# Two conditioning jobs of an encoder layer, each divided between TensorE and VectorE

## The chip, the cores and the metric

One NeuronCore of one Trainium2 chip runs the whole layer. The metric is the device time of one execution in microseconds. A *step* below is one 128x1024 slab of a weight matrix; a *unit* is one 512 KB load of the conditioning weights.

## The reference, cut to what matters

```python
c_act = jax.nn.silu(c)                                  # c: (1, 2048)
mod = c_act @ w_ada[0] + b_ada[0]                       # w_ada: (2048, 12288)
sh1, sc1, gt1, sh2, sc2, gt2 = jnp.split(mod, 6, axis=-1)
h = modulate(rms_norm(x, g_mix[0]), sh1, sc1)           # h * (1 + sc1) + sh1, 256 tokens x 2048
proj = h @ w_in[0] + b_in[0]                            # w_in: (2048, 5376)
# retention and windowed attention on proj, w_out, gt1, then the ConvGLU with sh2, sc2, gt2
fmod = c_act @ w_final_ada + b_final_ada                # shift and scale of the last norm
```

The conditioning vector `mod` is one row times a large matrix: 96 MB of weights for 12288 numbers. `h` needs `sh1` and `sc1` before `proj` can start on the features concerned.

## The kernel before, in words

Everything is float32 in memory. A product of the main path takes three TensorE passes over the halves of a split: ScalarE rounds a loaded slab into `whi` (`hi`, L643), VectorE writes the rest into `wlo` (`lo`, L999), TensorE multiplies (`passes`, L1535 to L1537). `whi` and `wlo` hold four steps each (RING = 4), so `hi(step)` waits until TensorE has done step - 4 or earlier. The raw slabs come through a ring of eight, loaded by SyncE (`load_step`, L365), each load issued once `lo` has freed or passed a given earlier step (for steps 16 to 37 once `lo(step - 6)` is done).

The projection is worked off while the conditioning vector is being made. The 2048 features are 16 tiles of 128 (`k`), and `STAGE_K` groups them into five stages: stage n needs the shift and scale of its own tiles, which conditioning *job* n gives. Stages 2 and 3, which the change touches, have twelve steps each: four of `att_queries(k)` and eight of `two_heads(stage, group, i)`, in four groups of query, heads, heads. In trace time stage 2 runs from about 83 to 129 us (steps 12 to 23 of the weights) and stage 3 from 129 to 174 us (steps 24 to 35). Each `two_heads` group fills PSUM banks 5 and 6; VectorE adds them to the running sum (`add_heads`, L1109) before the next group may write there (`bank_free`). So the heads of group 1 wait for `add_heads` of group 0, and so on.

A conditioning job 1, 2 or 3 makes 512 shifts and 512 scales. It has 16 units; unit k holds, in 128 partitions x 1024 columns, the rows of `w_ada` that belong to column k of `c_act`. TensorE takes them two at a time (`ada_pair(job, n)`, L1664): four fp32 matmuls of a 128x32 stationary tile `c_pad[:, k, :]`, recorded as eight instructions, in four column strips of the array. The strips collect in one PSUM bank; when eight pairs are done, VectorE adds the bias (`pe_rows`, L1031), TensorE sums the strips and turns them into columns (`sum_columns`, four matmuls against `pick`, L1608), and VectorE writes `mod_col` (`mod_cols`, L1049 and L1051), with which ScalarE modulates the next four tiles. Jobs 5 to 15 go another way: VectorE multiplies and accumulates a whole unit in one instruction (`ada_row`, L1009) and TensorE sums over partitions with a column of ones (L1611). The running sums lie in `acc`, four buffers of 128x1024.

In stages 2 and 3 the order written out by hand on TensorE is: in groups 0 and 1, query, pair, heads, pair, heads, pair; in group 2, query, heads, pair, heads, pair; in group 3, query, `sum_columns`, heads, heads. The order on VectorE, for i = 2 to 13: `lo_units(first + i)`, at i = 5, 8, 11 `add_heads` of groups 0, 1, 2, at i = 11 `pe_rows`, at i = 12 `mod_cols`; `first` is 12 and 24, so VectorE works at least two steps ahead.

GpSimd's queue issues the units, all from one instruction stream, in an order written out by hand (`pair_units`, `dve_unit`, L529), and clears and fills the bias of the `acc` buffers between them (`start_acc` L505, `next_acc`). Units of jobs 1 to 3 go round nine slots, eight of which (`k % 8`) these jobs use. A pair is issued when the pair four places earlier has been read:

```python
pool.wait_ge(ada_pe, PAIRS * job + n - (0 if job == JOB_SH2 else 3))
```

Of the kernel before, what the change touches and what calls it, by code (L numbers as in the profile page):

```python
# [25 lines left out]
ALU = mybir.AluOpType  # L26
ACT = mybir.ActivationFunctionType

P = 128
# [34 lines left out]
Y_PARTS = ((0, 0, GW), (0, GW, D), (1, 0, GW), (1, GW, GW + 512), (1, GW + 512, D))  # L64
ADA_PAIRS = 4


# [19 lines left out]
def build(nc, x, c, w_ada, b_ada, g_mix, w_in, b_in, sinks, w_out, g_ffn, w_up, w_conv, b_conv,  # L87
          w_down, w_final_ada, b_final_ada, g_final, rot, decay, masks, eye, out):
    ctx = ExitStack()
    with ctx:  # L90
# [177 lines left out]
        def rows_before(job):  # L268

            return KT * job - KT * JOB_DVE  # L270

# [4 lines left out]
        PAIRS = KT // 2  # L276

        def ada_slot(job, k):

            if job < 2:  # L280
                return k % (2 * RING)
            if job < JOB_SH2:
                return k % (2 * RING)
            if job == JOB_SH2:
                return PE_SLOTS[k % 2]
            n = rows_before(job) + k
            return n % RING
# [4 lines left out]
        def ada_value(job, k):  # L292

            if job < 2:
                return 16 * (2 * job + k // 8 + 1)
            if job < JOB_SH2:
                return 16 * (2 * job + k // (2 * RING) + 1)
            if job == JOB_SH2:
                return 16 * (2 * JOB_SH2 * (1 - k % 2) + k // 2 + 1)
            n = rows_before(job) + k  # L300
            return 16 * (2 * JOB_SH2 + n // RING + 1)

# [181 lines left out]
        def _(pool):  # L484
# [12 lines left out]
            def start_acc(job):  # L497

                a, col = acc[:, acc_of(job), :], column(job)
                before = [j for j in range(job) if acc_of(j) == acc_of(job)]  # L500
                if before and before[-1] < JOB_GT1:
                    pool.wait_ge(ada_red, summed(before[-1]))
                elif before:
                    pool.wait_ge(gt_ps, 2 * (before[-1] - JOB_GT1 + 1))
# [52 lines left out]
            def pair_units(job, n):  # L557

                if job == JOB_SH2 and n == 0:
                    pool.wait_ge(hlo_ready, KT)  # L560
                else:
                    pool.wait_ge(ada_pe, PAIRS * job + n - (0 if job == JOB_SH2 else 3))
                for k in (2 * n, 2 * n + 1):
                    load_unit(job, k, ada_slot(job, k))

            def dve_unit(n):

                job, k = JOB_DVE + n // KT, n % KT
                if n < RING:
                    pool.wait_ge(ada_pe, PAIRS * JOB_SH2 - RING + n // 2 + 1)  # L570
                else:
                    pool.wait_ge(ada_acc, n - RING + 1)
                load_unit(job, k, ada_slot(job, k))
# [23 lines left out]
            next_acc(3)  # L597
            for n in range(3):
                pair_units(2, n)
            next_acc(4)  # L600
            for n in range(3, PAIRS):
                pair_units(2, n)
            for n in range(3):
                pair_units(3, n)
            next_acc(5)
            for n in range(3, PAIRS):
                pair_units(3, n)
            for n in range(RING):
                dve_unit(n)
            pair_units(JOB_SH2, 0)  # L610
            next_acc(6)
            for n in range(RING, 3 * KT):
# [21 lines left out]
        def _(act):  # L634
# [168 lines left out]
            for p in range(P_WO):  # L803
# [9 lines left out]
                elif p == 25:  # L813

                    act.wait_ge(ada_pe, PAIRS * (JOB_SH2 + 1))
                    act.dma_start(dec, decay[:, :, 0:S]).then_inc(dec_in, 16)
                elif p in (30, 31):
                    exps(1, p - 30)
                elif 33 <= p < 37:
                    normalise(1, p - 33)  # L820
# [167 lines left out]
        def _(dve):  # L988
# [22 lines left out]
            def ada(job, k):  # L1011
# [5 lines left out]
                ada_row(acc[:, acc_of(job), :], ada_of_slot(ada_slot(job, k)), c_act[:, k:k + 1])  # L1017

            def first_rows(part):

# [5 lines left out]
            def pe_rows(job):  # L1026

                dve.wait_ge(bias_in, bias_value(job))
                dve.wait_ge(ada_pe, PAIRS * (job + 1))
                a = acc[:, acc_of(job), 0:512]  # L1030
# [117 lines left out]
            for stage in (2, 3):  # L1148
                first = AQ_STEPS[STAGE_K[stage][0]]
                for i in range(2, 14):  # L1150
                    lo_units(first + i)
                    if i in (5, 8, 11):
                        add_heads(stage, i // 3 - 1)
# [378 lines left out]
        def _(pe):  # L1532
# [68 lines left out]
            def sum_columns(job, bank, col0):  # L1601
# [3 lines left out]
                else:  # L1605
                    pe.wait_ge(ada_acc, rows_before(job + 1))
                for i in range(4 if job <= JOB_SH2 else 0):
                    last = nc.tensor.matmul(ps[:, bank, col0 + 2 * i:col0 + 2 * i + 2],  # L1608
                                            acc[:, acc_of(job), i * P:(i + 1) * P], pick[:, :], start=True, stop=True)
                for i in range(0 if job <= JOB_SH2 else 8):  # L1610
# [165 lines left out]
            for stage in (2, 3):  # L1776
                for group in range(4):
                    att_queries(STAGE_K[stage][group])
                    if group < 2:
                        ada_pair(stage, 3 * group)  # L1780
                    elif group == 3:
                        sum_columns(stage, ADA_BANK[stage], 0)
                    for i in range(2):
                        two_heads(stage, group, i)
                        if group < 3:
                            ada_pair(stage, 3 * group + i + (group < 2))
            keys_values(0)
# [253 lines left out]
```

## Time and profile before

| what | value |
|---|---|
| median of 3 runs | 1210.9 us (1209.73 to 1213.86) |
| the profiled execution's own time | 1214.22 us |
| its span, first to last instruction | 1212.5 us |
| mean granted TensorE clock | 0.988 |
| TensorE busy | 1176.8 us, 97% |
| VectorE busy | 899.0 us, 74% |

All times of rows are counted from the first instruction of the profiled execution, whose own time is 1.7 us above its span and 3.3 us above the median. "Busy" counts matmuls whose ends are modelled, so a full TensorE row says that its stream has no visible gap, and the distance between two starts is what an instruction group costs.

### The profile page before, as it was taken

The numbers are of one execution on the slowest core, as the hardware profiler recorded it, in microseconds if no ns is written. First come the engines' busy times: TensorE is split into PE (matmuls) and PEld (weight loads), VectorE is DVE, ScalarE is ACT, GpSimd is POOL, SyncE is SP. The second block draws the span as 40 slices with busy tenths as digits, with TensorE's granted clock in tenths as the row PEclk, the third lists the DMA queues.
The fourth block names the chain that finished last, engine by engine and source line by source line (L and its number), as shares of the span: only waits on it lengthen the run. The fifth ranks groups of instructions, "written<-read, shape, count | busy, mean of one in ns | idle before, by whom it ended". The sixth has DMA issues, their size and how long they took to land.

```text
span 1212.5 us, 19607 instructions
## 1 busy us (share of the span) xinstructions
PE 1176.8 (97%) x6800; PEld 986.4 (81%) x6800; DVE 899.0 (74%) x1111; ACT 656.3 (54%) x947; POOL 179.6 (15%) x307
## 2 busy tenths in 40 slices
PE   5999999999999999999999999999999999999995
PEld 3777898777888778888888888888888877888784
DVE  2444568998789887887887887877655666897886
ACT  5433344642754448565565665656655555555652
POOL 6342312221211110010111011000000000120101
PEclk9999999998999999999999999999999999999998
DMA  8999989998879984888888878885565557897841
GB/s 300 376 388 390 371 303 382 371 396 302 311 277 364 358 285 158 299 284 281 284 285 276 289 271 289 278 282 185 182 199 176 196 185 280 294 351 253 310 176 69
DMA packets 167478, 342.73 MB, mean 283 GB/s; under 512 B 10266, under 2 KB 103552, under 8 KB 166784
## 3 DMA queue, kind: packets, MB, share of 16 engines
q1 hardware_dynamic: 129072, 206.13, 49.1%
q0 software_dynamic: 37536, 134.30, 29.8%
q10 hardware_dynamic: 816, 1.58, 0.3%
q8 instruction: 34, 0.56, 0.2%
q14 instruction: 20, 0.16, 0.0%
HBM read 339.87 MB, written 2.10 MB: 282 GB/s over the span
## 4 chain that ended last, share of the span: by engine, by line
PE 83%; DMA 6%; DVE 5%; issue 2%; ACT 1%; POOL 1%; DVEq 0%; SPq 0%; ACTq 0%; POOLq 0%
PE ps L1559 27%; PE ps L1564 14%; PE ps L1535 13%; PE ps L1537 12%; PE ps L1536 12%; DMA ada_raw<-in_w_ada 3%; DVE acc L1009 2%; DMA raw<-in_w_in 2%; DMA arena<-in_w_ada 2%; PE ps L1664 2%; DVE wlo L999 1%; DVE xb L1333 1%; ACT whi L643 1%; PE ps L1611 0%; PE ps L1841 0%
## 5 line engine op out<-in xcount | busy, mean ns | idle before, releaser
L650 ACT ACTIVATE whi<-raw 128x1024 fp32r<-128x1024 f32 x256 | 271.6, 1062 | 286.4 <-PE ps L1564 180.6
L1004 DVE TENSOR_TENSOR wlo<-raw,whi 128x1024 fp32r<-128x1024 f32 x256 | 311.8, 1222 | 104.0 <-ACT whi L650 104.0
L1559 PE MATMUL ps<-hh,whi 128*128 128x512 f32 x1408 | 354.0, 393 | 0.0
L1559 PEld LDWEIGHTS ps<-hh,whi 128*128 128x128 f32 x1408 | 254.0, 189 | 45.9 <-issue 0.4
L1535 PE MATMUL ps<-whi,hh 128*128 128x512 f32 x608 | 243.1, 400 | 2.7 <-DVE wlo L999 1.4
L1537 PE MATMUL ps<-whi,hh 128*128 128x512 f32 x608 | 237.9, 391 | 0.0
L1536 PE MATMUL ps<-wlo,hh 128*128 128x512 f32 x608 | 237.7, 391 | 0.0
L643 ACT ACTIVATE whi<-raw 128x1024 fp32r<-128x1024 f32 x124 | 130.7, 1059 | 189.7 <-PE ps L1537 140.3
L1009 DVE SCALAR_TENSOR_TENSOR acc<-ada_raw,c_act,acc 128x1024 f32<-128x1024 f32 (+1 forms) x176 | 225.1, 1279 | 5.7 <-DMA ada_raw<-in_w_ada 5.0
L1564 PEld LDWEIGHTS ps<-hh,wlo 128*128 128x128 f32 x1408 | 192.1, 190 | 13.7
L999 DVE TENSOR_TENSOR wlo<-raw,whi 128x1024 fp32r<-128x1024 f32 x124 | 151.1, 1220 | 64.6 <-ACT whi L643 64.4
L1564 PE MATMUL ps<-hh,wlo 128*128 128x256 f32 x1408 | 196.3, 282 | 0.0
L1535 PEld LDWEIGHTS ps<-whi,hh 128*128 128x128 f32 x608 | 114.7, 189 | 34.3 <-issue 5.3
L1537 PEld LDWEIGHTS ps<-whi,hh 128*128 128x128 f32 x608 | 114.7, 189 | 24.7
L1536 PEld LDWEIGHTS ps<-wlo,hh 128*128 128x128 f32 x608 | 114.8, 189 | 23.5 <-issue 0.7
L529 POOL DMA_DIRECT2D ada_raw<-in_w_ada x136 | 76.3, 562 | 381.9 <-DVE acc L1009 328.5
L1535 PE MATMUL ps<-hh,whi 128*128 128x256 f32 x416 | 122.4, 294 | 3.2 <-DVE hh L1060 2.3
L1536 PE MATMUL ps<-hh,whi 128*128 128x256 f32 x416 | 118.5, 285 | 0.0
L1537 PE MATMUL ps<-hh,wlo 128*128 128x256 f32 x416 | 118.4, 285 | 0.0
L1535 PEld LDWEIGHTS ps<-hh,whi 128*128 128x128 f32 x416 | 81.5, 196 | 25.8 <-issue 25.8
L1536 PEld LDWEIGHTS ps<-hh,whi 128*128 128x128 f32 x416 | 81.7, 196 | 0.0
L1537 PEld LDWEIGHTS ps<-hh,wlo 128*128 128x128 f32 x416 | 81.6, 196 | 0.0
(161 smaller groups left out, 816.9 us busy)
## 6 DMA issues: line engine op xcount, KB each, us to landing
raw<-in_w_up SPq DMA_DIRECT2D x176, 512.0 KB, 4.4
ada_raw<-in_w_ada POOLq DMA_DIRECT2D x144, 512.0 KB, 7.2
raw<-in_w_down SPq DMA_DIRECT2D x44, 1024.0 KB, 6.5
ada_raw<-in_w_final_ada POOLq DMA_DIRECT2D x64, 512.0 KB, 5.3
raw<-in_w_in SPq DMA_DIRECT2D x52, 512.0 KB, 10.4
arena<-in_w_ada POOLq DMA_DIRECT2D x48, 512.0 KB, 9.1
raw<-in_w_in SPq DMA_DIRECT2D x16, 1024.0 KB, 8.8
raw<-in_w_out SPq DMA_DIRECT2D x16, 1024.0 KB, 8.1
```

The costliest lines, as they stand in the source:

```text
L529: pool.dma_start(dst, src).then_inc(ada_in[slot], 16)
L643: nc.scalar.activation(whi[:, step % RING, :], raw_of(step), ACT.Copy).then_inc(hi_ready, 1)
L650: nc.scalar.activation(whi[:, i % RING, :], raw_of(step0 + i), ACT.Copy).then_inc(hi_ready, 1)
L999: nc.vector.tensor_tensor(wlo[:, step % RING, :], raw_of(step), whi[:, step % RING, :], ALU.subtract).then_inc(lo_ready, 1)
L1004: nc.vector.tensor_tensor(wlo[:, i % RING, :], raw_of(step0 + i), whi[:, i % RING, :], ALU.subtract).then_inc(lo_ready, 1)
L1009: nc.vector.scalar_tensor_tensor(a, w, c_col, a, ALU.mult, ALU.add).then_inc(ada_acc, 1)
L1535: nc.tensor.matmul(out_ap, lhs[0], rhs[0], start=start, stop=False, skip_group_check=skip)
L1536: nc.tensor.matmul(out_ap, lhs[0], rhs[1], start=False, stop=False, skip_group_check=skip)
L1537: return nc.tensor.matmul(out_ap, lhs[1], rhs[0], start=False, stop=True, skip_group_check=skip)
L1559: nc.tensor.matmul(bank_of(m), whi[:, slot, tile(m, j)], hh[:, k0 + j, :, :].rearrange("p i s -> p (i s)"), start=start and j == 0, stop=F ...
L1564: last = nc.tensor.matmul(bank_of(m)[:, 0:S], wlo[:, slot, tile(m, j)], hhi[:, k0 + j, :], start=False, stop=True, skip_group_check=True)
L1664: last = nc.tensor.matmul(ps[row:row + 32, bank, :], c_pad[:, k, :], ada_of_slot(slot)[:, b * 512:(b + 1) * 512], start=n == 0, stop=True, ...
```

## The change

Jobs 2 and 3 are divided. TensorE takes units 0 to 7 as four pairs; VectorE takes units 8 to 15, one after each of `lo(first + 2)` to `lo(first + 9)`, into `acc` buffer 1 (`part_row`). `sum_columns` of these jobs gets eight more fp32 matmuls (128x128 of buffer 1 against one column of ones) that accumulate into the same eight PSUM columns. The order of TensorE in stages 2 and 3 becomes: in groups 0 and 1, query, heads, pair, heads, pair; in group 2, query, heads, heads; in group 3 as before. The eight slots are divided too: the pairs have four of them (so a pair is issued when the pair two places earlier has been read), VectorE's units the other four (a unit is issued when the row four places earlier is done). The order of GpSimd's queue becomes part, part, pair with both waits in one stream; the bias of buffer 1 for job 5 is moved behind job 3's sum, and the first four units of job 5 wait for rows of job 3.

```diff
--- before.py
+++ after.py
@@ -63,6 +63,7 @@
 LOOP = 8
 Y_PARTS = ((0, 0, GW), (0, GW, D), (1, 0, GW), (1, GW, GW + 512), (1, GW + 512, D))
 ADA_PAIRS = 4
+PART = 8
 
 
 JOB_SH2, JOB_SC2, JOB_GT1, JOB_GT2, JOB_FSC, JOB_FSH = 4, 6, 8, 10, 12, 14
@@ -267,20 +268,28 @@
 
         def rows_before(job):
 
-            return KT * job - KT * JOB_DVE
+            return KT * job - KT * JOB_DVE + 2 * PART
 
         def bias_value(job):
 
             return 32 * (job + 1) if type(job) is int and job <= JOB_SH2 else 16 * job + 16 * (JOB_DVE + 1)
 
         PAIRS = KT // 2
+
+        def pairs_before(job):
+
+            return PAIRS * job - PART // 2 * min(max(job - 2, 0), 2)
+
+        def part_before(job):
+
+            return PART * (job - 2)
 
         def ada_slot(job, k):
 
             if job < 2:
                 return k % (2 * RING)
             if job < JOB_SH2:
-                return k % (2 * RING)
+                return k % RING + (RING if k < KT - PART else 0)
             if job == JOB_SH2:
                 return PE_SLOTS[k % 2]
             n = rows_before(job) + k
@@ -294,11 +303,11 @@
             if job < 2:
                 return 16 * (2 * job + k // 8 + 1)
             if job < JOB_SH2:
-                return 16 * (2 * job + k // (2 * RING) + 1)
+                return 16 * (2 * job + k % PART // RING + 1)
             if job == JOB_SH2:
                 return 16 * (2 * JOB_SH2 * (1 - k % 2) + k // 2 + 1)
             n = rows_before(job) + k
-            return 16 * (2 * JOB_SH2 + n // RING + 1)
+            return 16 * (4 + n // RING + 1)
 
         def summed(job, part=1):
 
@@ -498,7 +507,9 @@
 
                 a, col = acc[:, acc_of(job), :], column(job)
                 before = [j for j in range(job) if acc_of(j) == acc_of(job)]
-                if before and before[-1] < JOB_GT1:
+                if job == JOB_DVE:
+                    pool.wait_ge(ada_red, summed(3))
+                elif before and before[-1] < JOB_GT1:
                     pool.wait_ge(ada_red, summed(before[-1]))
                 elif before:
                     pool.wait_ge(gt_ps, 2 * (before[-1] - JOB_GT1 + 1))
@@ -559,17 +570,22 @@
                 if job == JOB_SH2 and n == 0:
                     pool.wait_ge(hlo_ready, KT)
                 else:
-                    pool.wait_ge(ada_pe, PAIRS * job + n - (0 if job == JOB_SH2 else 3))
+                    pool.wait_ge(ada_pe, pairs_before(job) + n - (0 if job == JOB_SH2 else 1))
                 for k in (2 * n, 2 * n + 1):
                     load_unit(job, k, ada_slot(job, k))
 
+            def part_unit(job, i):
+
+                if job == 2 and i < RING:
+                    pool.wait_ge(ada_pe, pairs_before(2) - 3 + i // 2)
+                else:
+                    pool.wait_ge(ada_acc, part_before(job) + i - RING + 1)
+                load_unit(job, KT - PART + i, ada_slot(job, KT - PART + i))
+
             def dve_unit(n):
 
                 job, k = JOB_DVE + n // KT, n % KT
-                if n < RING:
-                    pool.wait_ge(ada_pe, PAIRS * JOB_SH2 - RING + n // 2 + 1)
-                else:
-                    pool.wait_ge(ada_acc, n - RING + 1)
+                pool.wait_ge(ada_acc, 2 * PART + n - RING + 1)
                 load_unit(job, k, ada_slot(job, k))
 
             nc.gpsimd.memset(c_pad[:, :, :], 0.0).then_inc(pad_zero, 1)
@@ -595,19 +611,23 @@
             next_acc(2)
             eight_units(1, 1)
             next_acc(3)
-            for n in range(3):
+            for i in range(RING):
+                part_unit(2, i)
+            for n in range(2):
                 pair_units(2, n)
-            next_acc(4)
-            for n in range(3, PAIRS):
+            for n in range(2, 4):
+                part_unit(2, 2 * n)
+                part_unit(2, 2 * n + 1)
                 pair_units(2, n)
-            for n in range(3):
-                pair_units(3, n)
-            next_acc(5)
-            for n in range(3, PAIRS):
+            for n in range(4):
+                part_unit(3, 2 * n)
+                part_unit(3, 2 * n + 1)
                 pair_units(3, n)
             for n in range(RING):
                 dve_unit(n)
+            next_acc(4)
             pair_units(JOB_SH2, 0)
+            next_acc(5)
             next_acc(6)
             for n in range(RING, 3 * KT):
                 for pair in range(1, PAIRS):
@@ -812,7 +832,7 @@
                     normalise(0, p - 14)
                 elif p == 25:
 
-                    act.wait_ge(ada_pe, PAIRS * (JOB_SH2 + 1))
+                    act.wait_ge(ada_pe, pairs_before(JOB_SH2 + 1))
                     act.dma_start(dec, decay[:, :, 0:S]).then_inc(dec_in, 16)
                 elif p in (30, 31):
                     exps(1, p - 30)
@@ -1016,6 +1036,18 @@
                     dve.wait_ge(ada_acc, rows_before(job) + k)
                 ada_row(acc[:, acc_of(job), :], ada_of_slot(ada_slot(job, k)), c_act[:, k:k + 1])
 
+            def part_row(job, i):
+
+                k, n = KT - PART + i, part_before(job) + i
+                w, col = ada_of_slot(ada_slot(job, k)), c_act[:, k:k + 1]
+                dve.wait_ge(ada_in[ada_slot(job, k)], ada_value(job, k))
+                if i:
+                    dve.wait_ge(ada_acc, n)
+                    ada_row(acc[:, 1, :], w, col)
+                else:
+                    dve.wait_ge(ada_red, summed(job - 1))
+                    nc.vector.tensor_scalar(acc[:, 1, :], w, col, None, ALU.mult).then_inc(ada_acc, 1)
+
             def first_rows(part):
 
                 dve.wait_ge(bias_in, bias_value(0))
@@ -1026,7 +1058,7 @@
             def pe_rows(job):
 
                 dve.wait_ge(bias_in, bias_value(job))
-                dve.wait_ge(ada_pe, PAIRS * (job + 1))
+                dve.wait_ge(ada_pe, pairs_before(job + 1))
                 a = acc[:, acc_of(job), 0:512]
                 nc.vector.tensor_tensor(a, ps[:, ADA_BANK[job], :], a, ALU.add).then_inc(ada_rows, 1)
 
@@ -1149,6 +1181,8 @@
                 first = AQ_STEPS[STAGE_K[stage][0]]
                 for i in range(2, 14):
                     lo_units(first + i)
+                    if i < 2 + PART:
+                        part_row(stage, i - 2)
                     if i in (5, 8, 11):
                         add_heads(stage, i // 3 - 1)
                     if i == 11:
@@ -1604,9 +1638,16 @@
                     pe.wait_ge(ada_rows, summed(job))
                 else:
                     pe.wait_ge(ada_acc, rows_before(job + 1))
+                if job in (2, 3):
+                    pe.wait_ge(ada_acc, part_before(job + 1))
                 for i in range(4 if job <= JOB_SH2 else 0):
                     last = nc.tensor.matmul(ps[:, bank, col0 + 2 * i:col0 + 2 * i + 2],
-                                            acc[:, acc_of(job), i * P:(i + 1) * P], pick[:, :], start=True, stop=True)
+                                            acc[:, acc_of(job), i * P:(i + 1) * P], pick[:, :], start=True,
+                                            stop=job not in (2, 3), skip_group_check=True)
+                    for b in range(2 if job in (2, 3) else 0):
+                        last = nc.tensor.matmul(ps[:, bank, col0 + 2 * i + b:col0 + 2 * i + b + 1],
+                                                acc[:, 1, (4 * b + i) * P:(4 * b + i + 1) * P], ones[:, 0:1],
+                                                start=False, stop=b == 1, skip_group_check=True)
                 for i in range(0 if job <= JOB_SH2 else 8):
                     last = nc.tensor.matmul(ps[:, bank, col0 + i:col0 + i + 1], acc[:, acc_of(job), i * P:(i + 1) * P],
                                             ones[:, 0:1], start=True, stop=True)
@@ -1776,14 +1817,12 @@
             for stage in (2, 3):
                 for group in range(4):
                     att_queries(STAGE_K[stage][group])
-                    if group < 2:
-                        ada_pair(stage, 3 * group)
-                    elif group == 3:
+                    if group == 3:
                         sum_columns(stage, ADA_BANK[stage], 0)
                     for i in range(2):
                         two_heads(stage, group, i)
-                        if group < 3:
-                            ada_pair(stage, 3 * group + i + (group < 2))
+                        if group < 2:
+                            ada_pair(stage, 2 * group + i)
             keys_values(0)
             keys_values(1)
             for k in STAGE_K[4]:
```

## Rows read from the trace of the kernel before

**Rows 1.** The page: busy time of two engines, and shares of the last chain by engine.
```profile
PE 1176.8 (97%) x6800; PEld 986.4 (81%) x6800; DVE 899.0 (74%) x1111; ACT 656.3 (54%) x947; POOL 179.6 (15%) x307
PE 83%; DMA 6%; DVE 5%; issue 2%; ACT 1%; POOL 1%; DVEq 0%; SPq 0%; ACTq 0%; POOLq 0%
```
**Rows 2.** Windows: length, busy PE, PEld, DVE, ACT, POOL, granted clock, DMA share, GB/s.
```profile
80.00:100.00 20.00, 19.49 (x156) 15.50 (x155) 9.78 (x14) 9.04 (x14) 7.12 (x10) 1.00 1.04 389
100.00:130.00 30.00, 29.68 (x239) 25.78 (x240) 16.04 (x23) 13.13 (x18) 8.52 (x12) 1.00 1.03 390
130.00:140.00 10.00, 10.00 (x82) 8.06 (x81) 5.38 (x6) 2.92 (x3) 2.81 (x4) 1.00 0.95 343
165.00:190.00 25.00, 25.00 (x211) 25.00 (x211) 20.18 (x24) 12.15 (x16) 5.31 (x10) 1.00 0.82 270
190.00:285.00 95.00, 90.24 (x655) 70.79 (x655) 85.52 (x120) 46.84 (x96) 21.34 (x41) 1.00 1.00 388
```
**Rows 3.** The chain that ended last, 60 to 260 us: start, length, what.
```profile
76.69 20.55 DMA raw<-in_w_in
97.26 1.07 ACT whi L643
...
99.49 0.70 DVE xb L1109
...
100.32 0.36 PE ps L1535
...
198.37 0.13 PE ps L1537
```
**Rows 4.** Timeline of PE in stages 2 and 3: start, length.
```profile
100.32 0.36 PE L1535 MATMUL ps<-hh,whi 128*128 128x256 f32 x1 [0.42 <-DVE xb L1109]
...
108.45 0.39 PE L1535 MATMUL ps<-hh,whi 128*128 128x256 f32 x1
...
122.41 1.05 PE L1608 MATMUL ps<-pick,acc 128*128 128x2 f32 x8
...
123.33 0.37 PE L1535 MATMUL ps<-hh,whi 128*128 128x256 f32 x1
...
129.17 0.28 PE L1535 MATMUL ps<-hh,whi 128*128 128x256 f32 x1
...
133.13 0.39 PE L1535 MATMUL ps<-hh,whi 128*128 128x256 f32 x1
...
137.21 0.39 PE L1535 MATMUL ps<-hh,whi 128*128 128x256 f32 x1
...
174.10 0.28 PE L1535 MATMUL ps<-hh,whi 128*128 128x256 f32 x1
```
**Rows 5.** The chain of waits: eight and sixteen instructions against one column of ones.
```profile
50.55 0.78 PE ps L1635 x8
...
287.88 2.19 PE ps L1611 x16
```
**Rows 6.** Timeline of DVE in stages 2 and 3, and in stage 4.
```profile
98.35 1.23 DVE L999 TENSOR_TENSOR wlo<-raw,whi 128x1024 fp32r<-128x1024 f32 x1 [1.98 <-ACT whi L643]
...
121.68 0.68 DVE L1031 TENSOR_TENSOR acc<-ps,acc 128x512 f32<-128x512 f32 x1
...
176.64 1.28 DVE L1009 SCALAR_TENSOR_TENSOR acc<-ada_raw,c_act,acc 128x1024 f32<-128x1024 f32 x1
177.84 1.22 DVE L999 TENSOR_TENSOR wlo<-raw,whi 128x1024 fp32r<-128x1024 f32 x1
...
195.59 1.22 DVE L999 TENSOR_TENSOR wlo<-raw,whi 128x1024 fp32r<-128x1024 f32 x1 [3.30 <-ACT whi L643]
```
**Rows 7.** Timeline of POOL: units issued (L529) and a buffer cleared (L505).
```profile
82.28 1.42 POOL L529 DMA_DIRECT2D arena<-in_w_ada  x2
87.58 1.41 POOL L529 DMA_DIRECT2D ada_raw<-in_w_ada  x2 [3.88 <-PE ps L1664]
...
174.51 0.97 POOL L505 MEMSET acc<- 128x1024 f32 x1
```
**Rows 8.** Landing of the units issued 78 to 110 us, then of those issued 138 to 156 us.
```profile
DMA to landing us min/median/max: 8.4/9.4/11.2
...
DMA to landing us min/median/max: 6.6/7.9/11.6
```
**Rows 9.** Waits from 76 to 124 us: engine, line, waited for; total, times, longest.
```profile
ACT whi L643 <- DMA raw<-in_w_in: 24.1, 11, 3.1
```

## The prediction

> **What bounds the kernel now.** The page comes first: TensorE is busy 97% of the span and holds 83% of the chain that ended last, while VectorE is busy 74% [rows 1]. Work taken from TensorE is worth something only where the chain runs through TensorE, so the next views are the chain and the windows of the two stages that change. Up to 100.32 us the chain is not on TensorE: it comes from the load of a weight slab, step 17, 20.55 us in flight, through ScalarE's rounding of it at 97.26, VectorE's `lo(17)` at 98.35 and the `add_heads` queued behind it at 99.49, which frees the banks for step 16 on TensorE at 100.32 [rows 3, 6]. From there to 198.37 us the chain is TensorE's [rows 3]. The windows say why: from 80 to 130 us the DMA engines are full (share 1.03 to 1.04, 389 GB/s) and TensorE is nearly full too, 19.49 of 20 and 29.68 of 30 us; from 130 us the transfers have caught up (0.95, later 0.82) and TensorE alone is full [rows 2]. ScalarE waits 24.1 us for slabs in stage 2 [rows 9]. So stage 3 is bound by TensorE, and stage 2 by TensorE with the transfers close behind.
>
> **What is removed: eight pairs.** A step behind a pair and before one costs 137.21 - 133.13 = 4.08 us [rows 4]. Stage 3 as a whole, twelve steps, eight pairs and a sum, takes 174.10 - 129.17 = 44.93 us [rows 4]; a step without a pair is 2.88 us (from 123.33 to 129.17, two steps, the first 0.08 longer because it comes behind fp32 matmuls: 5.84 [rows 4]). A pair therefore costs 4.08 - 2.88 = 1.20 us. Check: 12 x 2.88 + 8 x 1.20 = 44.2, and 0.8 to 0.9 for the sum makes 45.0. Stage 3 loses four pairs, 4.8 us. Stage 2 loses four as well, but two of them stood ahead of step 16, where TensorE then waits for the slab anyway [rows 3]. Only two, 2.4 us, are on the path.
>
> **What is added on TensorE: eight matmuls in each sum.** They are recorded as sixteen instructions. The same shape costs 0.78 us for eight [rows 5], so 1.6 us for sixteen, or 2.2 us as in the later sum of sixteen [rows 5]. I take 1.7, nearer to the first, because the clock is 1.00 in both stages [rows 2]. Two jobs: 3.4 us, range 3.2 to 4.4, all on the path. Without any new wait the change is thus worth 4.8 + 2.4 - 3.4 = 3.8 us.
>
> **What is added on VectorE: sixteen rows.** Row to next instruction is 177.84 - 176.64 = 1.20 us [rows 6], so 9.6 us in each stage. VectorE is busy 9.78 of 20 and 16.04 of 30 us in stage 2 [rows 2]; a step with its share of pairs takes TensorE over 3 us and VectorE needs 1.2 for `lo`, 1.2 for the row: hidden, except where `add_heads` stands behind a row. That is so for step 16, whose banks wait for `lo(17)`, then row 3, then `add_heads`: 1.2 us on the path if slab 17 lands when it did. But between 82.28 and 87.58 us four units are issued [rows 7] that the new order issues only after row 0 and row 1 (the slots are not free sooner), some 91 to 95 us. That is 2.1 MB, 5.4 us of all DMA engines at 389 GB/s [rows 2]; about half has come back by 97 us. Slab 17 lands 1.4 to 2.7 us earlier, 2.0 taken. Net: step 16 starts 0.8 us earlier, at 99.5 us; bounds 1.6 earlier (TensorE is ready no sooner) and 1.2 later.
>
> **What is moved: the units.** A pair now has four slots and stands behind two of VectorE's units in GpSimd's one queue. Pair 2 of stage 2 is behind the part that waits for row 1: with row 1 done at about 93 us, its second unit is issued at 94.4. Units issued here take 8.4 to 11.2 us to land, 9.4 in the middle [rows 8], so it is there at 103.8. TensorE wants it after step 16, at 99.5 + 2.9 = 102.4: a wait of 1.4 us. With pair 2 (1.2) and step 17 (2.9) TensorE is at 107.9. Pair 3 is behind the part that waits for row 3, done at 98.6 (before `add_heads`, 0.7, and 99.5); its second unit is issued at 100.0 and lands at 109.4, a wait of 1.5 us. Step 18 starts at 110.6 where it was 108.45 [rows 4]. From there four steps without pairs, 11.6 us, lead to the sum at 122.2, as now (122.41 [rows 4]). The sum can't be much earlier: `pe_rows`, 0.68 us from 121.68 [rows 6], is behind slab 23 and `add_heads`. It takes 0.9 + 1.7, so heads follow at 124.9 against 123.33: **stage 2 is 1.6 us longer.**
>
> In stage 3, starting at 130.8 us, row 1 is done at 136.7. Pair 2 is issued once pair 0 is done, by 138.3, lands 7.9 us later [rows 8] at 146.2 and is wanted at 147.6. Pair 3, issued at 142.6 behind row 3, lands at 150.5 and is wanted at 151.7. No wait by the middle landing, up to 2.5 us by the longest, 11.6 [rows 8]. So **stage 3 is shorter by 4.8 - 1.7 = 3.1 us.**
>
> Here a rule speaks against these waits: the Trainium skill, DMA: Bandwidth & Descriptors, section "Anatomy of one DMA — SWDGE (gpsimd) path", gives a transfer issued by GpSimd about 2.0 us plus its bytes at 436 GB/s, 3.2 us for a unit. By it both waits of stage 2 would be gone (2.9 us), the first rival below; the trace shows more than twice that wherever the engines are full, and the measurement decides here.
>
> **Behind the stages.** Buffer 1 is cleared for job 5 only after job 3's sum, and two more clearings with a wait for a bias between them stand in GpSimd's queue before the fifth unit of job 5; before, one clearing stood there at 174.51 [rows 7]. I estimate that unit 2 to 3 us late. VectorE's row 4 then waits as long, and behind it `lo`; TensorE is some steps behind, and VectorE has 3.30 us without work at 192 to 195.6 us [rows 6] that takes it up. If that cover were gone it would cost up to 3 us. DMA share 0.82 from 165 to 190 us [rows 2] leaves the transfers room to follow a small shift; from 190 to 285 us they are full again, 1.00 [rows 2], and could swallow a gain, not a loss.
>
> **The sum.** + 1.6 - 3.1 = -1.5 us. On the profiled execution, 1214.2 becomes 1212.7; on the median, which is 3.3 us lower, 1210.9 becomes about 1209.4.
>
> **The rivals.**
> 1. *Units land in time* (faster). No waits at pairs 2 and 3 and step 16 up to 1.6 us earlier: 3.8 + 1.6 = 5.4 us off, 1208.8 for the profiled execution and 1205.5 for the median. For it: no unit is issued from about 80 to 91 us, so that later ones may find the engines emptier. Against it: with 9.4 us landing and an issue hardly 8 us ahead the two waits follow from arithmetic, and the sum is held by slab 23.
> 2. *GpSimd's queue makes the pairs late* (slower). The point is the landing time: at 11.2 us in stage 2, and slab 17 no earlier than now, step 16 starts at 101.5; pair 2, issued at 95.1, waits 1.9 us, pair 3, issued at 102.3, 3.1 us. Step 18 then starts at 114.7, the sum 11.6 later at 126.3, and the heads behind it at 128.9, 5.6 us late. Stage 3, with 2.5 us of waiting, gains only 0.6. Together 5.0 us slower, 1215.9.
> 3. *Nothing passes through*: the transfers, full to 130 and again from 190 us [rows 2], bring the slabs at the times they do now, and 1.5 to 3 us won on TensorE are spent waiting: 1211.
>
> **How the numbers follow.** About 0.3%, 3.6 us, is what a measurement of this kernel can tell from no change. Forecast with its near neighbours (gain of 0 to 3.6 us) 0.42; rival 1 beyond 3.6 us 0.20; rival 3 and small losses 0.18; rival 2 beyond 3.6 us 0.20. Faster 0.20, same 0.60, slower 0.20. Range 1205.5 to 1216: from rival 1 to rival 2.
>
> **What would show it.** the pairs' line with 192 instead of 256 instructions; 14 more instructions of the accumulating row (the first of each job only multiplies); sums of about 2.6 us near 122 and 164 us; TensorE idle before two pairs between 100 and 110 us, released by a load of `w_ada`; step 18 later than 108.45 us, and stage 3 about 41.8 us long with no idle time. The prediction is wrong if landing in stage 2 leaves 9.4 us by more than 1.5, if a sum costs over 3.1 us, if slab 17 doesn't move, or if VectorE comes to wait for its own units and holds `lo` back.

## The result, and the profile after

The changed kernel takes 1223.36 us (median of 4 runs, 1222.0 to 1224.02) against 1210.56 us for the kernel before: ratio 1.0096, 95% interval 1.0069 to 1.0123. It is slower by 8 to 15 us where 1.5 us faster was forecast, and outside the range.

The page of the changed kernel, the lines of [rows 1]. TensorE has 32 instructions fewer (64 of the pairs gone, 32 in the sums new) and 1.7 us less busy time in a span that is 8.7 us longer. (The medians differ by 12.8 us: the profiled execution of the kernel before was 3.3 us above its median, that of the changed kernel 0.5 us below.)

```profile
PE 1175.1 (96%) x6768; PEld 988.2 (81%) x6768; DVE 916.7 (75%) x1127; ACT 656.5 (54%) x947; POOL 179.7 (15%) x307
PE 83%; DMA 7%; DVE 5%; issue 2%; ACT 1%; POOL 1%; DVEq 0%; SPq 0%; ACTq 0%; POOLq 0%
```

The windows of the changed kernel, columns as in [rows 2]:

```profile
80.00:100.00 20.00, 17.53 (x140) 15.25 (x140) 14.72 (x20) 11.06 (x15) 4.50 (x7) 1.00 1.04 390
100.00:130.00 30.00, 24.57 (x163) 19.86 (x161) 16.10 (x16) 5.47 (x6) 6.77 (x10) 0.89 1.02 383
130.00:140.00 10.00, 10.00 (x86) 10.00 (x86) 4.93 (x10) 6.66 (x11) 0.00 (x0) 1.00 0.39 117
140.00:165.00 25.00, 21.98 (x161) 16.31 (x160) 20.37 (x20) 6.36 (x6) 7.49 (x12) 1.00 0.91 322
```

TensorE was busy 29.68 of 30 us from 100 to 130 us [rows 2] and is now busy 24.57, at a granted clock of 0.89 instead of 1.00. From 130 to 140 us the DMA engines move 117 GB/s where they moved 343 [rows 2]. TensorE's timeline through the two stages, to be held against [rows 4], says where:

```profile
99.48 0.37 PE L1569 MATMUL ps<-hh,whi 128*128 128x256 f32 x1 [1.06 <-DVE xb L1141]
...
103.33 1.05 PE L1705 MATMUL ps<-arena,c_pad 128*32 128x512 f32 x4 [0.73 <-DMA arena<-in_w_ada]
105.36 1.05 PE L1705 MATMUL ps<-arena,c_pad 128*32 128x512 f32 x4 [0.98 <-DMA arena<-in_w_ada]
106.35 0.39 PE L1569 MATMUL ps<-hh,whi 128*128 128x256 f32 x1
...
112.14 1.05 PE L1705 MATMUL ps<-arena,c_pad 128*32 128x512 f32 x4 [2.64 <-DMA arena<-in_w_ada]
114.27 1.92 PE L1705 MATMUL ps<-arena,c_pad 128*32 128x512 f32 x4 [1.08 <-DMA arena<-in_w_ada]
116.12 0.58 PE L1569 MATMUL ps<-hh,whi 128*128 128x256 f32 x1
...
120.94 0.28 PE L1569 MATMUL ps<-hh,whi 128*128 128x256 f32 x1
...
132.17 0.37 PE L1569 MATMUL ps<-hh,whi 128*128 128x256 f32 x1
...
138.02 0.28 PE L1569 MATMUL ps<-hh,whi 128*128 128x256 f32 x1
...
162.34 1.05 PE L1705 MATMUL ps<-arena,c_pad 128*32 128x512 f32 x4 [1.50 <-DMA arena<-in_w_ada]
164.12 1.05 PE L1705 MATMUL ps<-arena,c_pad 128*32 128x512 f32 x4 [0.73 <-DMA arena<-in_w_ada]
165.10 0.39 PE L1569 MATMUL ps<-hh,whi 128*128 128x256 f32 x1
...
185.14 0.28 PE L1569 MATMUL ps<-hh,whi 128*128 128x256 f32 x1
```

Three things are to be seen. Step 16 starts at 99.48 us, as forecast. The late pairs shown are recorded as two groups of four instructions, one for each unit, with a gap ahead of both, released by the load of that unit (pair 2 of stage 3 waits 0.80 us for its second unit alone). And pair 3 of stage 2 with its waits holds TensorE from the end of step 17, near 109.3, to 116.12 us. Stage 3 begins at 138.02 instead of 129.17 and ends at 185.14 instead of 174.10 [rows 4]: 11.0 us are lost by then.

The chain that ended last now runs, just ahead of 114 us, through exactly the queue that was in question (start, length, what):

```profile
97.45 1.29 DVE acc L1029
98.74 0.29 issue
99.03 0.70 POOL ada_raw L540
99.73 0.69 POOL arena L540
100.42 13.80 DMA arena<-in_w_ada
114.22 0.04 issue
114.27 1.92 PE ps L1705 x4
```

VectorE's row 3, then GpSimd's issue of VectorE's unit, then of the pair's, then 13.80 us of transfer, then TensorE. GpSimd's timeline shows the pause and the burst behind it, against two units at 82.28 and two at 87.58 in [rows 7]:

```profile
77.04 2.80 POOL L540 DMA_DIRECT2D arena<-in_w_ada  x4 [2.67 <-PE ps L1705]
90.53 0.71 POOL L540 DMA_DIRECT2D ada_raw<-in_w_ada  x1 [10.69 <-DVE acc L1049]
93.69 0.71 POOL L540 DMA_DIRECT2D ada_raw<-in_w_ada  x1 [2.45 <-DVE acc L1029]
94.39 0.71 POOL L540 DMA_DIRECT2D arena<-in_w_ada  x1
...
99.72 1.41 POOL L540 DMA_DIRECT2D arena<-in_w_ada  x2
...
141.60 0.71 POOL L540 DMA_DIRECT2D ada_raw<-in_w_ada  x1 [23.69 <-DVE acc L1049]
```

Eight units are issued in the 10 us from 90.53, one each 1.4 us, where before it was two each 4.1 us. Ahead of stage 3 GpSimd waits 23.69 us for row 0 of the fourth job. Its last unit has landed at 130.0 us, and SyncE, whose slabs wait for VectorE's splits and so for TensorE, issues a single one between 130 and 140 us: the DMA engines run nearly dry.

### The profile page after: what moved, and what is told of

Its sections match the earlier page's. It is cut to its first block, busy times and chain, and to the rows that moved or that the text cites. A ratio compares the mean times of both kernels' runs of the same rounds, so it can differ in the third digit from the quotient of the medians.

```text
span 1221.2 us, 19577 instructions
## 1 busy us (share of the span) xinstructions
PE 1175.1 (96%) x6768; PEld 988.2 (81%) x6768; DVE 916.7 (75%) x1127; ACT 656.5 (54%) x947; POOL 179.7 (15%) x307
## 4 chain that ended last, share of the span: by engine, by line
PE 83%; DMA 7%; DVE 5%; issue 2%; ACT 1%; POOL 1%; DVEq 0%; SPq 0%; ACTq 0%; POOLq 0%
PE ps L1593 27%; PE ps L1598 14%; PE ps L1569 13%; PE ps L1571 12%; PE ps L1570 12%; DMA arena<-in_w_ada 4%; DVE acc L1029 2%; DMA raw<-in_w_in 2%; DMA ada_raw<-in_w_ada 2%; PE ps L1705 1%; DVE wlo L1019 1%; ACT whi L663 1%; DVE xb L1367 1%; PE ps L1652 0%; PE ps L1880 0%
## 5 line engine op out<-in xcount | busy, mean ns | idle before, releaser
L1029 DVE SCALAR_TENSOR_TENSOR acc<-ada_raw,c_act,acc 128x1024 f32<-128x1024 f32 (+1 forms) x190 | 242.9, 1279 | 7.9 <-DMA ada_raw<-in_w_ada 7.1
L1569 PEld LDWEIGHTS ps<-whi,hh 128*128 128x128 f32 x608 | 114.3, 188 | 34.4 <-issue 5.3
## 6 DMA issues: line engine op xcount, KB each, us to landing
raw<-in_w_in SPq DMA_DIRECT2D x52, 512.0 KB, 10.7
```

Of the source, the lines that this page charges most:

```text
L1029: nc.vector.scalar_tensor_tensor(a, w, c_col, a, ALU.mult, ALU.add).then_inc(ada_acc, 1)
L1569: nc.tensor.matmul(out_ap, lhs[0], rhs[0], start=start, stop=False, skip_group_check=skip)
```

## The experiments

Theory L: the units of pairs 2 and 3 are issued too late, because they stand behind VectorE's rows in one queue with only four slots, and TensorE stands idle for them. Rivals: R, VectorE's rows hold back the splitting of the slabs; D, the transfers as a whole are the limit. Lengths below: stage 2 from the heads behind job 1's sum (80.26 us before, 79.76 changed) to stage 3's first step; before 48.9 us, changed 58.3; stage 3 before 44.9, changed 47.1. Every ratio is to the kernel before, run beside the kernel in question; its median was 1210.56 to 1211.68 us from one comparison to the next, so a difference in microseconds between two of them can be off by about 1 us.

### Late pairs

```diff
-                        if group < 2:
-                            ada_pair(stage, 2 * group + i)
+                        if group == 0:
+                            ada_pair(stage, i)
+                        elif group == 2 and i:
+                            ada_pair(stage, 3)
```
and `ada_pair(stage, 2)` behind the query of group 2.

> The changed kernel with pairs 2 and 3 of each shared job later in TensorE's order: pair 2 behind the query of group 2, pair 3 behind the second heads of group 2 (before: both in group 1). Nothing else moves. Theory L (the units of pairs 2 and 3 are issued too late behind VectorE's units in GpSimd's queue, and TensorE stands idle for them): the waits before these pairs all but vanish, stage 3 starts 6 to 9 us earlier than in the changed kernel, and the time falls by 8 to 12 us to some 1212 to 1215. Rival R (VectorE's rows hold back the splitting of the slabs): no change, 1223. Rival D (the transfers as a whole are the limit): under 3 us gained.

Measured: 1209.56 us, ratio 0.9979 (0.9963 to 0.9994). The waits at pairs are gone from the trace, though the units land no sooner. Landing of those issued from 97 to 102 us, in this kernel:

```profile
DMA to landing us min/median/max: 10.2/14.0/14.7
```

The same late units cost nothing if TensorE asks for them two or three steps later (pair 3's second unit lands at 114.51 us and is used at 114.59). Stage 3 takes 172.42 - 130.46 = 41.96 us, the 41.8 of the forecast. L holds, though the gain is 13.8 us where it expected 8 to 12; R and D fall, since all rows and all loads are still there. Only a move in TensorE's order turns a loss of 1% into a gain of 0.2%.

### Pairs first in GpSimd's queue

```diff
-                part_unit(2, 2 * n)
-                part_unit(2, 2 * n + 1)
                 pair_units(2, n)
+                part_unit(2, 2 * n)
+                part_unit(2, 2 * n + 1)
```
and the same for the fourth job.

> The changed kernel with each pair's two units issued ahead of VectorE's two units in GpSimd's queue, where they stood behind. Theory L: pairs 2 and 3 of stage 2 are issued about 3 and 4 us earlier and wait that much less, in both stages; 1223 becomes 1214 to 1218. Rival B (the units land late because ten of them are issued in 10 us after a pause, whatever their order): the waits only move from the pairs to the rows, and less than 3 us is gained. Rival R: no change.

Measured: 1218.35 us, ratio 1.0061 (1.0038 to 1.0085), 5 us better than changed. The wait moves from TensorE to VectorE, which now waits four times, up to 5.5 us, for its own units (waits from 76 to 190 us: total, times, longest):

```profile
DVE acc L1029 <- DMA ada_raw<-in_w_ada: 14.7, 4, 5.5
PE ps L1705 <- DMA arena<-in_w_ada: 3.8, 4, 1.3
```

In the changed kernel these rows are 3.2 us (2 times) and 8.5 us (7 times). The gain lies between the two expectations. About a third of what the waits cost (5.0 of 14.7 us, the next experiment) is the order of VectorE's units and the pairs in the queue.

### No wait at the late pairs

```diff
+                    held = job in (2, 3) and n >= 2
+                    if not held:
-                    pe.wait_ge(ada_in[slot], ada_value(job, k))
+                        pe.wait_ge(ada_in[slot], ada_value(job, k))
```
and the moving operand of a held pair is `c_pad`. TensorE waits for the held units only ahead of the sum. The kernel leaves these eight units out of the conditioning vector.

> The changed kernel in which pairs 2 and 3 of the two shared jobs multiply a constant tile that is always there; their units are still loaded, and TensorE waits for them only at the sum. It leaves these eight units out of the conditioning vector. Theory L: all of the idle time before these pairs is gone, about 5.4 us in stage 2, 3 us in stage 3 and what the fallen clock cost; 1223 becomes 1209 to 1212. Rival R: it stays above 1218, since the rows remain. Rival D: slabs arrive no sooner and stage 2 ends within 2 us of where it did.

Measured: 1208.65 us, ratio 0.9975 (0.9962 to 0.9987): 14.7 us below the changed kernel. TensorE has no gap from 100 to 130 us:

```profile
100.00:130.00 30.00, 30.00 (x237) 28.06 (x237) 19.71 (x26) 12.23 (x16) 6.07 (x9) 0.94 1.03 389
```

So the waits and what follows from them are the whole loss. It is also a measured value of the change without them: 0.25% faster, 3.0 us (1.6 to 4.6), near the 3.8 us of the prediction's sum without new waits, though this trace has the clock at 0.94 in the stretch.

### Narrow rows

```diff
-                    ada_row(acc[:, 1, :], w, col)
+                    ada_row(acc[:, 1, 0:8], w[:, 0:8], col)
```
(and the first row likewise). The kernel leaves the rest of VectorE's share out.

> The changed kernel with VectorE's sixteen rows cut to 8 of 1024 columns, all waits and loads kept. It leaves the rest of VectorE's share out. Theory L: the rows themselves cost nearly nothing, since the pairs wait for loads; but each load behind a row is issued about 1 us earlier, so 1 to 3 us are gained, 1220 to 1222. Rival R: the loss goes with them, 1211 to 1214.

Measured: 1219.79 us, ratio 1.0082 (1.0065 to 1.0099), 3.6 us less than changed, with overlapping intervals. TensorE still waits, for units that release it at 103.1, 105.2 and 114.1 us; in the changed kernel it was at 103.3, 105.4 and 114.3. R falls as a main cause. Pair 3's units are issued 2.0 us earlier (97.77 against 99.72 us) and land no earlier.

### A fill under the wait

```diff
+                        if stage == 2 and group == 1 and i:
+                            for _ in range(5):
+                                nc.tensor.matmul(ps[:, 7, :], ident[:, :], c_pad[:, :, :].rearrange("p k c -> p (k c)"),
+                                                 start=True, stop=True, skip_group_check=True)
```

> The changed kernel with five fp32 matmuls of the identity against a constant tile, into a PSUM bank that nobody reads, ahead of pair 3 of stage 2, where TensorE stands idle. Theory C (the half clock from 114 to 120 us follows from the idle time before it): the fill hides under the wait, the clock stays at 1.00, step 18 starts where it did and step 19 some 2 us sooner behind it; stage 3 starts 2 to 3.5 us earlier. Rival: the clock falls at about this time whatever TensorE does, and stage 3 starts where it did or later.

The granted clock in the changed kernel, and in this one:

```profile
114.00:116.00 2.00, 1.73 (x4) 0.19 (x4) 0.00 (x0) 0.00 (x0) 0.15 (x1) 0.50 1.04 387
116.00:118.00 2.00, 2.00 (x11) 1.88 (x10) 0.00 (x0) 0.00 (x0) 1.40 (x2) 0.50 1.04 390
118.00:120.00 2.00, 2.00 (x11) 2.00 (x11) 0.00 (x0) 0.00 (x0) 0.00 (x0) 0.50 1.03 389
```

```profile
114.00:120.00 6.00, 5.18 (x39) 4.10 (x38) 0.00 (x0) 0.72 (x1) 1.40 (x2) 1.00 1.04 390
130.00:134.00 4.00, 4.00 (x23) 4.00 (x22) 2.50 (x6) 3.08 (x7) 0.00 (x0) 0.57 0.59 176
```

The first fence is the changed kernel, the second the one with the fill. With the fill, which takes 4.45 us from 108.80 us, the 1.2 GHz level (0.50) is gone at 114 us, and step 18 takes 2.97 instead of 4.82 us. The sum starts 1.9 us earlier, at 127.66. But the low level comes behind the sum instead, at 130 us, and takes most of that back: stage 3 starts at 137.59, where it was 138.02. There is one time, 1221.34 us, which can't be told from 1223. So half of the expectation holds in this one execution: with the idle time filled, the clock does not fall at 114 us. The gain is missing, because it then falls behind the sum.

### Early rows in stage 2

```diff
             mod_cols(1, ADA_BANK[1], 0)
+            for i in range(2):
+                part_row(2, i)
```
and rows 2 to 7 behind the splits of steps 14 to 19.

> The changed kernel with VectorE's rows of stage 2 two places earlier: rows 0 and 1 straight behind the second job's columns, near 81 us, the others behind the splits of steps 14 to 19. Theory B (the units of pairs 2 and 3 land late because GpSimd stops for 10.7 us at row 0 and then issues eight units in 10 us, one each 1.2 us, where the full engines land one each 2.1 us): the landing of pair 3's units falls from 12.4 to 13.8 us to some 9, step 18 starts 4 to 6 us earlier, the clock does not fall there, and the time is 5 to 9 us below 1223. Rival (a longer landing comes from the four slots alone): under 2 us gained, since pair 3 is still issued only behind pair 1.

Measured: 1219.22 us, ratio 1.0068 (1.0045 to 1.0092), 4 us less. Pair 3 is issued at 95.77 instead of 99.72 us and lands at 108.2 and 110.4 instead of 112.1 and 114.3, so its landing time did not fall:

```profile
DMA to landing us min/median/max: 11.0/13.8/15.3
```

(units issued from 95 to 101 us). The intervals of this kernel and the changed one overlap. The clock does not fall at pair 3, but in the profiled execution it does behind the sum, from 126.8 us. Theory B, that spreading the issue brings landing back to 9 us, is not confirmed: six units, pair 3's the last of them, are still issued between 91.7 and 96.5 us. A kernel without any burst was not tried.

### The sum alone, on the kernel before

```diff
+                    for b in range(2 if job in (2, 3) else 0):
+                        last = nc.tensor.matmul(ps[:, bank, 8 + 2 * i + b:8 + 2 * i + b + 1],
+                                                acc[:, acc_of(job), i * P:(i + 1) * P], ones[:, 0:1],
+                                                start=True, stop=True, skip_group_check=True)
```

> The kernel before, with the eight one-column matmuls added to the sums of jobs 2 and 3 (on a buffer that is there, into columns that nobody reads) and nothing else of the change. The forecast's term: 1.7 us each, 3.4 us in all, 1214. Theory C2: one or two stretches at half clock on top, 2 to 3.4 us each, so 1216 to 1221.

Measured: 1217.28 us, ratio 1.0045 (1.0028 to 1.0063): 3.4 to 7.6 us. The sums take 2.69 and 2.75 us from start to the next step, 0.8 to 0.9 before. Behind the second one the clock falls:

```profile
168.00:170.00 2.00, 2.00 (x21) 2.00 (x19) 0.00 (x0) 1.06 (x1) 0.00 (x0) 1.00 0.83 220
170.00:172.00 2.00, 2.00 (x13) 2.00 (x13) 1.02 (x3) 0.63 (x2) 0.00 (x0) 0.61 0.17 66
172.00:174.00 2.00, 2.00 (x11) 2.00 (x11) 1.27 (x3) 1.94 (x5) 0.00 (x0) 0.53 0.23 28
```

Steps 34 and 35 behind it take 7.20 us instead of the 5.84 of the two steps from 123.33 us before [rows 4]. This longer sum costs its instructions, 1.8 to 1.9 us each time, and in the profiled execution 1.4 us at the low clock on top, behind one of the two sums. How often that happens in the other five executions isn't known.

### The sum in two parts

Late pairs, and VectorE's part of the sum ahead of the last query of the stage, TensorE's part behind it:

```diff
                 for group in range(4):
+                    if group == 3:
+                        sum_part(stage)
                     att_queries(STAGE_K[stage][group])
```
(The waits and banks that go with it are left out here.) In the first version every column of VectorE's part set the start flag, and that kernel leaves part of the sum out; the second sets it once for the bank and leaves nothing out.

> The kernel with the late pairs and the sum cut in two: the sixteen instructions on VectorE's part stand ahead of the last query of the stage, the eight on TensorE's part behind it, both into a bank of their own. Theory C2 (a 2.6 us stretch of twenty-four matmuls of one or two columns brings the half clock seen from 120.6 to 127.6 us in the kernel with late pairs, as it does behind the sum of jobs 4 and 5 in the kernel before): no half clock in stage 2, 2 to 3.4 us gained, ratio to before some 0.996. Rival (the clock falls there for another reason): the same half clock within 5 us, ratio 0.998.

> The kernel with late pairs and the divided sum once more, with one start flag for the bank, so that both parts add up. The same instructions and waits: ratio 0.996 again, and a fall of the clock of no more than 4 us in stage 2.

Measured: 1207.4 us, ratio 0.9962 (0.9948 to 0.9976), and 1207.98 us, 0.9972 (0.9960 to 0.9984). In the profiled execution of the first the clock falls all the same, right behind the sixteen instructions:

```profile
118.00:122.00 4.00, 4.00 (x23) 4.00 (x23) 1.32 (x2) 0.00 (x0) 0.00 (x0) 0.57 1.04 395
```

In that of the second it stays at 1.00 through both stages; yet that execution, 1212.84 us, was the longest of its twelve. The intervals of both overlap that of the late pairs alone. That the divided sum helps is not shown.

### Early rows, late pairs and the divided sum together

No edit of its own: the three above in one kernel.

> Late pairs, divided sum, and VectorE's rows of stage 2 two places earlier, together. If the early rows help beside the late pairs (units spread better), ratio 0.993 to 0.995. If they only bring slab 17 and step 16 later, as they did alone (100.6 against 99.5 us), and no pair waits any more, 0.996 to 0.998.

Measured: 1209.45 us, ratio 0.9982 (0.9970 to 0.9994). Once no pair waits, early rows bring nothing that can be seen; step 16 starts at 100.05 us. In the profiled execution the clock falls twice in stage 2, from 89.0 and from 119.7 us, each time for 3.4 us.

### One job at a time

The third job alone shared, with the changed order in stage 2, and the fourth alone:

```diff
-                        if i < 2 + PART:
+                        if stage == 2 and i < 2 + PART:
```
(and the counts, slots and TensorE's and GpSimd's orders of the other job as before).

> Only the third job is shared, with the changed kernel's order of TensorE and GpSimd in stage 2; the fourth job and stage 3 are as before. Stage 2 was 9.3 us longer in the changed kernel and stage 3 2.2 us longer, so theory L expects 7 to 10 us above before, 1218 to 1221, with the waits at pairs 2 and 3 of stage 2 and the half clock behind them. Rival (the loss needs both jobs, through the one second sum): under 5 us.

> Only the fourth job is shared, with the changed kernel's order in stage 3; the third job and stage 2 are as before. The first four units of VectorE's part and two pairs are on their way in stage 2, but unit 4 of its part still waits for row 0 behind the split of step 26. Theory L: waits of 2 to 4 us at pairs 2 and 3 against 3.1 us saved, so 1210 to 1215. The forecast's walk of stage 3 (no waits): 1208. With a half clock behind the longer sum, 2 us more.

Measured: third alone 1220.3 us, ratio 1.0084 (1.0063 to 1.0105); fourth alone 1214.31 us, 1.0036 (1.0021 to 1.0051). Their sum is 1.2%, in the interval of the whole. In the third alone, stage 2 takes 58.2 us and stage 3 44.9; pair 3 waits as in the changed kernel:

```profile
111.89 1.05 PE L1714 MATMUL ps<-arena,c_pad 128*32 128x512 f32 x4 [2.64 <-DMA arena<-in_w_ada]
114.02 1.92 PE L1714 MATMUL ps<-arena,c_pad 128*32 128x512 f32 x4 [1.07 <-DMA arena<-in_w_ada]
```

In the fourth alone stage 2 is as before and stage 3 takes 46.7 us, with gaps ahead of both units of pair 3:

```profile
153.11 1.05 PE L1707 MATMUL ps<-arena,c_pad 128*32 128x512 f32 x4 [1.41 <-DMA arena<-in_w_ada]
154.89 1.05 PE L1707 MATMUL ps<-arena,c_pad 128*32 128x512 f32 x4 [0.72 <-DMA arena<-in_w_ada]
```

Each stage makes its own loss; the shared second sum between the jobs isn't needed for it.

## Why the prediction was wrong

**What failed** is the step "units issued here take 8.4 to 11.2 us to land, 9.4 in the middle" and its twin with 7.9 us in stage 3. The landing time was read from a kernel that issues two units each 4.1 us and carried over, as if it were a property of the transfer, to one that stops for 10.7 us and then issues eight in 10 us. Pair 3's second unit took 13.80 us in stage 2 and 14.0 in stage 3. I named the landing time as the point on which rival 2 turns, but set its upper end at 11.2, the longest before, so that the bound was too low as well. The sign that I gave for it, a landing more than 1.5 us off 9.4, is there.

**Why it took 13.80 us.** The landing of each single unit can be read from the traces. In every kernel here GpSimd's units land, from 76 to 190 us, in the order in which they were issued, and while the engines are full, about one each 2.1 us: pair 3's two units and the five before them at 101.16, 103.29, 105.32, 107.44, 109.69, 112.09 and 114.22 us, a mean distance of 2.2; in the kernel before, from 98.59 to 111.41 us, 2.1. So the landing time is mostly a place in the line. Of the units issued in the changed kernel from 95.67 us on, the one with three loads of GpSimd's still under way took 9.65 us, those with four 10.7, the one with five 12.4, and pair 3's second unit, with six, 13.80. In the kernel before there were never more than five from 78 to 110 us. With six ahead it was 13.84 us in the kernel with early rows and 14.0 in stage 3: that is why spreading the issue a little did not lower the landing time. During the pause the line ran down to one load, and none landed between 93.12 and 98.10 us.

**Point by point in stage 2** (forecast, measured). Step 16: 99.5, 99.48; 0.5 us of that is luck, since the stage began that much earlier in this execution, and from its start the step came 0.3 us sooner instead of 0.8. (Slab 17 was 2.9 us earlier, but `lo(17)` then stood behind row 2.) Step 17, behind pair 2: 105.0, 106.35; GpSimd issued the second unit 1.3 us later than taken, and it landed in 9.7 us. Step 18, behind pair 3: 110.6, 116.12; 4.9 us of it are the landing at 114.27 instead of 109.4 (0.4 of these the later issue), the rest the second half of the pair at the low clock. Step 18 itself: 2.9, 4.82 us, the fallen clock, which no term had. The sum: 2.6, 2.60. Stage 2 became 9.4 us longer instead of 1.6.

**Stage 3**: forecast 41.8 us, measured 47.12. Both late pairs were issued behind rows that had waited for the third job's sum. Pair 3's second unit took 14.0 us where the forecast had 7.9 and 11.6 at most, and released TensorE at 164.12 us, where it had been free at 160.8. The terms on TensorE were right: with the waits out of the way the stage takes 41.96 us.

**Right**: a pair is 1.20 us, the new sum is 2.6 us, two pairs ahead of step 16 are worth nothing, and a gain near 3.8 us without the new waits. Behind the stages nothing is added, as taken: the main path is 11.0 us late from 178 to 261 us. What the two longer sums cost the whole kernel is less sure than the term of 3.4 us: 3.4 to 7.6 us, by the sum alone on the kernel before. The rule of the Trainium skill that I set beside the trace (DMA: Bandwidth & Descriptors, "Anatomy of one DMA — SWDGE (gpsimd) path"; by its fit, given per DMA, an estimate of 3.2 us for a unit) was even further off: 13.80 us.

**The whole**: the stages explain 9.35 + 2.2 = 11.5 us, and the interval of the whole is 8 to 15 us. The two profiled executions differ by less, 8.7 us: between 277 and 296 us of the kernel before, 2.4 of the 11.0 us come back, 1.6 of them across the sums of jobs 4 and 5, where the kernel before spent 6.8 us at the low clock (from 289.1) and the changed one 3.4. That is luck of the execution as far as is known. With the waits out of the way, by the experiment on them, 14.7 us are regained. Rival 2 had the right mechanism and chance 0.20, at less than half its size.

**Left open**: what sets the 2.1 us from one landing to the next, in an estimate 250 GB/s of the 389 that all loads together reach, and whether a kernel without the pause would have kept pair 3 in time.

## What to carry to other kernels

A landing time belongs to the issue pattern in which it was read: count the loads of the same queue that are still under way, the new one with them, and price each at the distance between two landings (here seven loads at some 2 us). When a change halves the look-ahead of a ring or puts another engine's wait ahead of a load in the same queue, count how many transfers are issued in the burst behind the wait, and place the consumer by the last of them. Where a loss is a late load, first try to move the consumer: here two calls moved by two or three steps took the kernel from 1% slower to 0.2% faster, with the same loads in the same order.

## What was unexpected of the hardware

The granted clock of TensorE fell to the 1.2 GHz level from 113.5 to 120.3 us, behind 2.64 us of idle time ahead of pair 3's first unit and within the 1.08 us ahead of its second. It also fell in several kernels at or right behind a sum, sixteen to twenty-four recorded instructions of one or two columns in fp32, in which the profile shows TensorE as busy all the time: with late pairs from 120.7 us, at the end of the sum that starts at 118.86.

```profile
118.00:120.00 2.00, 1.85 (x16) 1.65 (x16) 1.94 (x3) 0.39 (x1) 0.00 (x0) 1.00 1.03 389
120.00:128.00 8.00, 8.00 (x44) 8.00 (x44) 3.15 (x7) 4.95 (x10) 0.00 (x0) 0.57 1.03 389
```

The kernel before has the same at the sums of jobs 4 and 5, from 289.1 to 295.9 us. It does not follow in every execution: the changed kernel has none at its two new sums, the fourth job alone and the second version of the divided sum have none in these stages, while the first version and the kernel with all three changes have one. Why a stretch that counts as busy is followed by the low level stays open.
